# One sum of squares in the first mixer's opening, and three reordered mixers, in a six-stage block on one core

## The chip, the cores and the metric

The kernel runs on one core of one Trainium2 chip. The metric is the device time of one execution in microseconds (us). A core has five engines with a queue of instructions each: TensorE (PE: matmuls, PEld: the weight loads that go with them), VectorE (DVE), ScalarE (ACT), GpSimd (POOL) and SyncE (SP), which starts the DMAs here. Each engine runs its own queue strictly in order and waits on semaphores for the others.

## The reference, cut to what matters

The input x is 512 tokens by 1024 channels in float32. It goes through six stages, each of the form x = x + rmsnorm(stage(rmsnorm(x))):

```
even : retention (4 heads) and stick-breaking attention (8 heads), gated, projected back
odd  : hgrn2 (4 heads, chunked decays) and a convolution + RG-LRU recurrence, gated, projected
diff : differential attention (8 score units per pair of heads), a 31-tap depthwise conv + layernorm
ffn0 : gated feed-forward, 1024 -> 2816 -> 1024
ssm  : a diagonal complex state-space scan and latent attention (6 heads)
ffn1 : as ffn0
rms_norm(x) = x * rsqrt(mean(x*x over channels) + 1e-6) * w
```

The four stages that are not feed-forward are the mixers.

## The kernel before, in words

x lies channel-major: eight blocks (k = 0 to 7) of 128 channels by 512 tokens. Every projection is a product of a 128 by 128 weight tile with such a block, made at nearly full precision from three fp32r matmuls: high by high, high by low and low by high (L889 to L891; in the openings L906, L910, L917). High parts are rounded by ACT (`hh` from x, L1059; `wh` from the raw weights, L1034), low parts are the differences, made by DVE (`hl`, L1125) and POOL (`wl`, L3165, four instructions for a slot). Weights come as a stream of slots of eight tiles (512 KB). Slot n is loaded by SP, rounded by ACT, split by POOL; rings of three slots hold `raw`, `wh` and `wl`, so a step that starts a slot (`STARTS`) also makes ACT round, and POOL split, the slot two places on.

A stage's opening takes the blocks of x as they come. For block k, ACT makes `hh` and the square of x (L1064), DVE makes `hl`, PE does the stage's first three or four products with this block. The norm's factor is applied later, when results leave PSUM, so the products need not wait for it. For the factor, the squares must be summed over all channels: PE multiplies by a 128 by 128 matrix of ones (plain float32) into bank 7, and ACT then takes Ln and Exp (`rs`, L1067, L1069); the evictions `e` by DVE wait for that. There are two forms of this sum:

- the stages named in `ADDING` (odd, ffn0, ssm, ffn1): the squares go to `y` in the arena, DVE adds them up there (steps `sa` 1 to 7, L1132), and PE multiplies the one total (L978);
- the other stages (even, diff): PE multiplies each square by itself, eight matmuls that add up in bank 7 (L988). In even they stand in groups of four, three and one, behind the products of blocks 3, 6 and 7 (`SQUARES`), and the squares lie in four buffers of `nrm`.

The order of all this is written out by hand: `steps_even()` and its fellows list the steps of a stage, every engine walks the same list and emits its own part of each step. On top of that a table, `AHEAD`, moves single steps ahead of others: an entry `(step, of)` takes `step` out and puts it directly before `of`. It had 79 entries for even, 158 for odd, 214 for diff and 146 for ssm. A move changes the place of the step in every queue at once, and with it the order in which that engine reaches its waits.

Steps that come up below. In odd: `hf`/`hq` are projections; `fa`, `fb`, `fc` turn hf into log decays (ACT L1943 to L1947 and L1954 to L1959, DVE L1799 to L1803); `bd 3` loads ACT's sigmoid table (L1894) and sets a mask on DVE (L1716, L1718); `lf` is DVE L1783; `t` are the 8 by-token products of the values (L960 to L962), the first of which needs PSUM banks 0 to 3, thus the evictions of hq by DVE (L1691); `h0` and `hl` are the score products by head and level (L1636), which need DVE (L1809, L1833, L1815) and POOL (L2037). In diff: `ra` and `rb` rotate q and k (PE L2116, DVE L2208 and L2214, POOL L2408), `r1` are scores (L2131) that need the rotated k, `fn` is the conv branch's norm and gate (DVE L2278, L2280, L2283). In ssm: `an` is a block of six POOL instructions on angles (L3115 to L3125).

Of the kernel before, what the change touches and what calls it, by code (L numbers as in the profile page):

```python
# [18 lines left out]
KT = D // 128  # L19
# [114 lines left out]
SQUARES = {3: (0, 1, 2, 3), 6: (4, 5, 6), 7: (7,)}  # L134
# [6 lines left out]
def opening(gs):  # L141

    even = gs == OPENS["even"]

    def at(kind, k):
        return [(kind, k) if even or k >= NB else (kind, k, 1)] if k < KT else []

    out = at("nx", 0) + at("hi", 0) + at("nx", 1)
    for k in range(KT):
        out += at("lo", k) + at("hi", k + 1) + at("nx", k + 2)  # L150
        out += [("w", g, k) for g in gs]
        if gs in LATER:
            out += ADDED.get(k, [])
        else:
            out += [("sq", n) for n in (SQUARES.get(k, ()) if even else (k,))]
    return out + [("rs",)] * (gs not in LATER)
# [6 lines left out]
ADDING = ("odd", "ffn0", "ssm", "ffn1")  # L163
# [54 lines left out]
def steps_even():  # L218
    sq, sk = ([(g, j) for j in range(4)] for g in ("sq", "sk"))
    out = opening(OPENS["even"]) + merge(group(sq[3], 8), [("e", g) for g in sq[:3]]) + [("e", sq[3]), ("rt",)] + groups(sk, 8, "e")  # L220
# [168 lines left out]
def steps_ssm():  # L389
# [29 lines left out]
    for n in range(0, 24, 2):  # L419
# [78 lines left out]
    "diff": [  # L498
# [292 lines left out]
def program(nc, io):  # L791
    with ExitStack() as ctx:
# [61 lines left out]
        def square_at(stage):  # L854
            return [y[:, k, :] for k in range(KT)] if stage in ADDING else sqr + [nrm[:, 4, :], nrm[:, 5, :]] if stage == "even" else sqr
# [109 lines left out]
        def pe_norms(e, stage, step):  # L965
# [7 lines left out]
            elif kind == "sq":  # L973
# [7 lines left out]
                if k == 0:  # L981
                    claim(e, 7)
                    if stage == "even":
                        e.wait_ge(s_mats, 16)
# [2366 lines left out]
```

## Time and profile before

| | us |
|---|---|
| median of 3 runs (1749.95 to 1752.95) | 1750.78 |
| the profiled execution | 1755.67 |
| its span, first to last instruction | 1753.9 |
| PE busy in it | 1699.9 |
| DVE / ACT / POOL busy | 961.7 / 769.7 / 949.0 |

Read from it first who is busy (PE, by far), then whose waits cost: only time in which PE idles, or runs at the lower granted clock, can be won without taking work off PE. Stages follow each other: odd runs from about 304 to 546 us, diff from 546 to 791, ssm from 1148 to 1372.

### The profile page before, as it was taken

The page shows a single profiled execution, that of the slowest core. Times are in us where ns is not written, and L with a number is a line of the kernel's source. Part 1 is how long each engine was busy: PE and PEld are TensorE (multiplying, and loading weights), DVE is VectorE, ACT ScalarE, POOL GpSimd, SP SyncE. Part 2 cuts the span into 40 slices and gives each one's busy share as a digit, 9 for nine tenths or more (in the row PEclk, how much of TensorE's full clock was granted, in tenths as well). Part 3 has the DMA queues.
Part 4 walks back from the last instruction along what each step waited for, and adds up shares of the span by engine and source line. Part 5 has one row for each costly group of instructions (what it writes and reads, how often), then busy time and mean ns, then how long its engine had stood idle before and what let it go on. Part 6 is the DMA issues. An engine that isn't in the chain of part 4 may idle for free.

```text
span 1753.9 us, 21148 instructions
## 1 busy us (share of the span) xinstructions
PE 1699.9 (97%) x7871; PEld 1324.0 (75%) x7871; DVE 961.7 (55%) x1504; ACT 769.7 (44%) x1314; POOL 949.0 (54%) x1108
## 2 busy tenths in 40 slices
PE   9999999998999999899999999999999999999997
PEld 6767668776878776687888888875457888888886
DVE  2033555779966898747614313369786752132344
ACT  4254675477475334754322222354335533222232
POOL 4433224678964463235656656569354565565662
PEclk9999999999999999899999999999999999999998
DMA  5221112222112221022322222221001222222221
GB/s 210 83 84 61 36 49 96 95 73 84 49 37 86 83 85 49 26 83 97 108 97 96 96 96 97 96 72 48 13 24 49 85 96 101 92 97 100 96 96 69
DMA packets 39702, 139.96 MB, mean 80 GB/s; under 512 B 4528, under 2 KB 4656, under 8 KB 39472
## 3 DMA queue, kind: packets, MB, share of 16 engines
q1 hardware_dynamic: 39600, 138.61, 23.4%
q8 instruction: 63, 1.03, 0.2%
q14 instruction: 39, 0.32, 0.1%
HBM read 136.50 MB, written 2.10 MB: 79 GB/s over the span
## 4 chain that ended last, share of the span: by engine, by line
PE 81%; DVE 11%; ACT 4%; issue 2%; POOL 1%; DMA 0%; SPq 0%; DVEq 0%; ACTq 0%
PE ps L889 19%; PE ps L891 18%; PE ps L890 18%; PE ps L910 1%; PE ps L960 1%; PE ps L917 1%; PE ps L962 1%; PE ps L961 1%; DVE ps L1101 1%; PE ps L1178 1%; PE ps L1176 1%; PE ps L1177 1%; PE ps L906 1%; PE ps L1312 1%; PE ps L1636 1%
## 5 line engine op out<-in xcount | busy, mean ns | idle before, releaser
L3165 POOL TENSOR_TENSOR wl<-raw,wh 128x256 fp32r<-128x256 f32 x988 | 801.3, 842 | 710.0 <-ACT wh L1034 704.0
L1034 ACT ACTIVATE wh<-raw 128x1024 fp32r<-128x1024 f32 x246 | 259.4, 1056 | 479.9 <-PE ps L891 441.0
L889 PE MATMUL ps<-hh,wh 128*128 128x512 f32 x1028 | 414.6, 403 | 2.4 <-ACT arena L1472 0.8
L891 PE MATMUL ps<-hh,wl 128*128 128x512 f32 x1028 | 401.3, 390 | 0.0
L890 PE MATMUL ps<-hl,wh 128*128 128x512 f32 x1028 | 401.0, 390 | 0.0
L889 PEld LDWEIGHTS ps<-hh,wh 128*128 128x128 f32 x1028 | 193.5, 188 | 56.2 <-issue 12.0
L890 PEld LDWEIGHTS ps<-hl,wh 128*128 128x128 f32 x1028 | 193.5, 188 | 42.8 <-issue 4.5
L891 PEld LDWEIGHTS ps<-hh,wl 128*128 128x128 f32 x1028 | 193.4, 188 | 41.0
L889 PE MATMUL ps<-mh,wh 128*128 128x512 f32 x540 | 220.0, 407 | 3.4 <-DVE ml L2955 1.4
L891 PE MATMUL ps<-mh,wl 128*128 128x512 f32 x540 | 211.2, 391 | 0.0
L890 PE MATMUL ps<-ml,wh 128*128 128x512 f32 x540 | 210.9, 391 | 0.0
L889 PEld LDWEIGHTS ps<-mh,wh 128*128 128x128 f32 x540 | 102.0, 189 | 32.9 <-issue 3.3
L891 PEld LDWEIGHTS ps<-mh,wl 128*128 128x128 f32 x540 | 101.6, 188 | 21.7
L890 PEld LDWEIGHTS ps<-ml,wh 128*128 128x128 f32 x540 | 101.9, 189 | 21.1 <-issue 2.2
L2469 DVE TENSOR_TENSOR ml<-arena,mh 128x512 fp32r<-128x512 f32 x44 | 36.3, 825 | 101.2 <-ACT mh L2500 101.2
L2458 DVE TENSOR_TENSOR arena<-ps,nrm 128x512 f32<-128x512 f32 x44 | 30.3, 688 | 107.0 <-PE ps L891 107.0
L2456 DVE TENSOR_TENSOR arena<-ps,nrm 128x512 f32<-128x512 f32 x44 | 29.9, 680 | 107.1 <-PE ps L891 94.3
L2238 DVE SCALAR_TENSOR_TENSOR ps<-arena,vec,ps 128x512 f32<-128x512 f32 x116 | 79.9, 748 | 0.2
L1125 DVE SCALAR_TENSOR_TENSOR hl<-x,vec,hh 128x512 fp32r<-128x512 f32 (+1 forms) x63 | 45.1, 720 | 28.2 <-ACT hh L1059 28.2
L1076 ACT ACTIVATE nrm<-arena 128x256 f32<-128x256 f32 (+1 forms) x68 | 34.1, 501 | 56.2 <-DVE arena L1142 56.0
L960 PE MATMUL ps<-wh,hh 128*128 128x512 f32 x128 | 52.2, 408 | 2.8 <-DVE arena L1691 1.9
L1176 PE MATMUL ps<-mh,wh 128*128 128x256 f32 x184 | 53.1, 289 | 0.0
(497 smaller groups left out, 2746.7 us busy)
## 6 DMA issues: line engine op xcount, KB each, us to landing
raw<-in_w SPq DMA_DIRECT2D x246, 512.0 KB, 3.3
x<-in_x SPq DMA_DIRECT2D x8, 256.0 KB, 8.3
out<-x SPq DMA_DIRECT2D x8, 256.0 KB, 2.0
arena<-in_rope SPq DMA_DIRECT2D x3, 512.0 KB, 4.7
arena<-in_dec SPq DMA_DIRECT2D x1, 1024.0 KB, 6.3
mats<-in_mats SPq DMA_DIRECT2D x1, 576.0 KB, 9.4
raw<-in_w SPq DMA_DIRECT2D x2, 256.0 KB, 3.7
arena<-in_lw SPq DMA_DIRECT2D x1, 512.0 KB, 4.1
```

Source lines behind the costliest of these rows:

```text
L889: e.matmul(ps[b][:], a, xh, start=first, stop=False)
L890: e.matmul(ps[b][:], a, xl, start=False, stop=False)
L891: e.matmul(ps[b][:], l, xh, start=False, stop=final).then_inc(pe.sem, pe.up(*step))
L960: e.matmul(ps[i][:], hh[:, k, cut(i)], a, start=(k == 0), stop=False)
L1034: e.activation(wh[:, n % NHL, :], raw[:, n % NRAW, :], ACT.Copy).then_inc(rounded.sem, rounded.up(n))
L1076: e.activation(sqr[d % 2][:, c], y[:, d, c], ACT.Square).then_inc(act.sem, act.up("oe", d, *half))
L1125: e.scalar_tensor_tensor(out=hl[:, k, c], in0=x[:, k, c], scalar=V(PRE[stage], k), in1=hh[:, k, c].bitcast(F32), op0=MUL, op1=SUB).then_in ...
L1176: e.matmul(ps[b][:, cols(h)], a, mh[:, r, cols(h)], start=(k == 0), stop=False)
L2238: e.scalar_tensor_tensor(out=yb[:, j, :] if q == 30 else conv_in[j], in0=du[:, j, q:q + T], scalar=V("dww", 4 * q + j), in1=conv_in[j], op ...
L2458: e.tensor_tensor(f_up[f % 2], ps[bank(stage, ("fu", f))][:], rb_pre, MUL).then_inc(dve.sem, dve.up("e", ("fu", f)))
L2469: e.tensor_tensor(ml[:, i, :], f_up[f % 2], mh[:, i, :].bitcast(F32), SUB).then_inc(dve.sem, dve.up("mixed", f))
L3165: e.tensor_tensor(wl[:, n % NHL, cut(i, 2)], raw[:, n % NRAW, cut(i, 2)], wh[:, n % NHL, cut(i, 2)].bitcast(F32), SUB).then_inc(split.sem, ...
```

## The change

First, even joins the stages in `ADDING`. Its squares go to the arena, DVE adds them up, and PE multiplies once by ones. The steps `sa` stand as in the other stages: `sa 1` behind block 3, `sa 2` behind block 5, `sa 3` to `sa 7` behind block 7. `sq 7` and `rs` follow directly on the opening. In odd, ffn0, ssm and ffn1 a group of eight products stands between the last `sa` and `sq 7`; in even none does. Second, the tables of moves of odd, diff and ssm are other ones (184, 243 and 164 entries); that of even stays. The stream of weights and every operation of the three mixers stay the same, only their order in the queues differs (and with it where ACT's tables are loaded).

```diff
-SQUARES = {3: (0, 1, 2, 3), 6: (4, 5, 6), 7: (7,)}
 ADDED = {3: [("sa", 1)], 5: [("sa", 2)], 7: [("sa", k) for k in range(3, KT)]}
...
         if gs in LATER:
             out += ADDED.get(k, [])
         else:
-            out += [("sq", n) for n in (SQUARES.get(k, ()) if even else (k,))]
+            out += [("sq", k)]
...
-ADDING = ("odd", "ffn0", "ssm", "ffn1")
+ADDING = ("even", "odd", "ffn0", "ssm", "ffn1")
...
-    out = opening(OPENS["even"]) + merge(group(sq[3], 8), [("e", g) for g in sq[:3]]) + ...
+    out = opening(OPENS["even"]) + [("sq", KT - 1), ("rs",)] + merge(group(sq[3], 8), [("e", g) for g in sq[:3]]) + ...
...
     "odd": [
-        (('w', ('p', 6), 3), ('hn3', 2)), (('hn4', 1), ('w', ('p', 6), 2)), (('hn4', 0), ('hn4', 1)), (('hn3', 1), ('w', ('p', 6),
...
-            return [y[:, k, :] for k in range(KT)] if stage in ADDING else sqr + [nrm[:, 4, :], nrm[:, 5, :]] if stage == "even" else sqr
+            return [y[:, k, :] for k in range(KT)] if stage in ADDING else sqr
...
                 if stage in ADDING:
                     claim(e, 7)
+                    if stage == "even":
+                        e.wait_ge(s_mats, 16)
+                        e.wait_ge(consts.sem, consts[EXACT[-1]])
                     e.wait_ge(dve.sem, dve["sa", k])
                     e.matmul(ps[7][:], M("ones"), y[:, 0, :], start=True, stop=True).then_inc(pe.sem, pe.up("sq", k))
```

**Place one, the opening of even.** PE before, behind the products of block 5: the products of block 6, three sums, the products of block 7, the last sum, and then group sq 3 (L889 on).

```order
L906 MATMUL ps<-hh,wh 128x512 x3
L910 MATMUL ps<-hl,wh 128x512 x3
L917 MATMUL ps<-hh,wl 128x512 x3
L988 MATMUL ps<-nrm,mats 128x512 x3
L906 MATMUL ps<-hh,wh 128x512 x3
L910 MATMUL ps<-hl,wh 128x512 x3
L917 MATMUL ps<-hh,wl 128x512 x3
L988 MATMUL ps<-nrm,mats 128x512
L889 MATMUL ps<-hh,wh 128x512
```

PE now at the same place (line numbers have moved by about 20):

```order
L926 MATMUL ps<-hh,wh 128x512 x3
L930 MATMUL ps<-hl,wh 128x512 x3
L937 MATMUL ps<-hh,wl 128x512 x3
L926 MATMUL ps<-hh,wh 128x512 x3
L930 MATMUL ps<-hl,wh 128x512 x3
L937 MATMUL ps<-hh,wl 128x512 x3
L1001 MATMUL ps<-arena,mats 128x512
L909 MATMUL ps<-hh,wh 128x512
```

Seven of the eight sums are gone, and the one that is left reads the arena. DVE before, from its first instruction on, and then now:

```order
L3141 MEMSET small 128x1 x3
L1337 MEMSET nrm 128x256
L1125 SCALAR_TENSOR_TENSOR hl<-x,vec,hh 128x512 x8
L1350 SCALAR_TENSOR_TENSOR mh_scratch<-ps,nrm 128x512 x4
L1137 COPY small<-ps 128x4
```

```order
L3160 MEMSET small 128x1 x3
L1356 MEMSET nrm 128x256
L1144 SCALAR_TENSOR_TENSOR hl<-x,vec,hh 128x512 x4
L1151 TENSOR_TENSOR arena<-arena 128x512
L1144 SCALAR_TENSOR_TENSOR hl<-x,vec,hh 128x512 x2
L1151 TENSOR_TENSOR arena<-arena 128x512
L1144 SCALAR_TENSOR_TENSOR hl<-x,vec,hh 128x512 x2
L1151 TENSOR_TENSOR arena<-arena 128x512 x5
L1369 SCALAR_TENSOR_TENSOR mh_scratch<-ps,nrm 128x512 x4
```

Seven adds have come in, five of them in a row behind the last `hl`.

**Place two, ACT in odd, where the log decays are made.** Before, from the table load of `bd 3` on:

```order
L1894 ACT_TABLE_LOAD
L1943 ACTIVATE nrm<-arena 128x512
L1945 ACT_TABLE_LOAD
L1945 ACTIVATE nrm<-nrm 128x512
L1947 ACT_TABLE_LOAD
L1947 ACTIVATE nrm<-nrm,small 128x512
L1936 ACTIVATE mh<-mh_scratch 128x512
L1034 ACTIVATE wh<-raw 128x1024 x2
L1954 ACT_TABLE_LOAD
L1954 ACTIVATE arena<-arena,small 128x512
L1955 ACTIVATE nrm<-nrm,small 128x512
L1957 ACTIVATE nrm<-nrm 128x512
```

Now, from the last `fa` on (L1962 to L1966 are the former L1943 to L1947, L1973 to L1978 the former L1954 to L1959):

```order
L1962 ACTIVATE nrm<-arena 128x512
L1964 ACTIVATE nrm<-nrm 128x512
L1966 ACTIVATE nrm<-nrm,small 128x512
L1053 ACTIVATE wh<-raw 128x1024
L1973 ACTIVATE arena<-arena,small 128x512
L1974 ACTIVATE nrm<-nrm,small 128x512
L1976 ACTIVATE nrm<-nrm 128x512
L1978 ACTIVATE nrm<-nrm,small 128x512
L1955 ACTIVATE mh<-mh_scratch 128x512
L1053 ACTIVATE wh<-raw 128x1024 x2
L1973 ACTIVATE arena<-arena,small 128x512
```

`bd 3` now stands among the tanh steps `lt`, ahead of `la`, and with it the eight loads between here and the first `hd` are gone.

**Place three, DVE in diff, where the last q and k are rotated.** Before (L2208 and L2214 are `ra` and `rb`, the first of each q, the second k; L2246 belongs to the softmax rows):

```order
L2208 TENSOR_TENSOR arena<-arena 128x512
L2278 TENSOR_TENSOR arena<-arena,nrm 128x512
L2280 TENSOR_SCALAR arena<-arena,vec 128x512
L2283 SCALAR_TENSOR_TENSOR arena<-arena 128x512
L2214 TENSOR_TENSOR arena<-ps,arena 128x512
L2278 TENSOR_TENSOR arena<-arena,nrm 128x512
L2280 TENSOR_SCALAR arena<-arena,vec 128x512
L2278 TENSOR_TENSOR arena<-arena,nrm 128x512
L2280 TENSOR_SCALAR arena<-arena,vec 128x512
L2208 TENSOR_TENSOR arena<-arena 128x512
L2214 TENSOR_TENSOR arena<-ps,arena 128x512
```

Now (19 is to be added to the line numbers):

```order
L2227 TENSOR_TENSOR arena<-arena 128x512
L2265 TENSOR_REDUCE small<-ps 128x1 x2
L2227 TENSOR_TENSOR arena<-arena 128x512
L2297 TENSOR_TENSOR arena<-arena,nrm 128x512
L2299 TENSOR_SCALAR arena<-arena,vec 128x512
L2233 TENSOR_TENSOR arena<-ps,arena 128x512
L2297 TENSOR_TENSOR arena<-arena,nrm 128x512
L2299 TENSOR_SCALAR arena<-arena,vec 128x512
L2302 SCALAR_TENSOR_TENSOR arena<-arena 128x512 x2
L2233 TENSOR_TENSOR arena<-ps,arena 128x512
```

Between the two `rb` stood two rounds of `fn` 0 and one `ra`; now one round of `fn` 0 and two `fn` 2 stand there. On PE the product `ra` of k followed directly on that of q; now a score unit and the first values (`r1 11`, `v1 0`) stand between them. In ssm, POOL's last five blocks `an` 3 to 7 now follow each other without a weight split in between, and the split of the slot that begins with tile (p 2, 2) comes behind `an 7`; before it came ahead of `an 6`.

## Rows read from the trace of the kernel before

**Rows 1.** The page: busy time and share by engine; the chain's shares.

```profile
PE 1699.9 (97%) x7871; PEld 1324.0 (75%) x7871; DVE 961.7 (55%) x1504; ACT 769.7 (44%) x1314; POOL 949.0 (54%) x1108
PE 81%; DVE 11%; ACT 4%; issue 2%; POOL 1%; DMA 0%; SPq 0%; DVEq 0%; ACTq 0%
```

**Rows 2.** Windows of odd, diff, ssm: length, busy by engine, granted clock, DMA.

```profile
304.00:546.00 242.00, 232.94 (x1183) 191.53 (x1183) 192.84 (x274) 150.60 (x262) 175.15 (x183) 0.99 0.20 68
546.00:791.00 245.00, 233.54 (x1082) 174.45 (x1081) 191.15 (x338) 123.37 (x245) 100.66 (x127) 0.98 0.21 69
1148.00:1372.00 224.00, 210.59 (x982) 140.25 (x983) 171.91 (x249) 103.03 (x211) 128.34 (x118) 0.98 0.13 43
```

**Rows 3.** The chain of waits in even's opening: start us, length us, what.

```profile
17.78 3.43 PE ps L988 x8
21.21 0.69 PE ps L906 x3
...
27.36 2.58 PE ps L988 x6
...
32.00 0.86 PE ps L988 x2
```

**Rows 4.** Timeline of the opening: start, length, engine, line, what, idle before.

```profile
12.72 3.76 POOL L3165 TENSOR_TENSOR wl<-raw,wh 128x256 fp32r<-128x256 f32 x4 [3.64 <-ACT wh L1034]
...
18.67 0.63 ACT L1064 ACTIVATE nrm<-x 128x512 f32<-128x512 f32 x1 [1.35 <-PE ps L988]
...
22.22 0.75 DVE L1125 SCALAR_TENSOR_TENSOR hl<-x,vec,hh 128x512 fp32r<-128x512 f32 x1 [0.38 <-ACT hh L1059]
...
23.61 1.04 ACT L1034 ACTIVATE wh<-raw 128x1024 fp32r<-128x1024 f32 x1
...
24.73 5.57 POOL L3165 TENSOR_TENSOR wl<-raw,wh 128x256 fp32r<-128x256 f32 x8 [4.67 <-ACT wh L1034]
```

**Rows 5.** The adds of squares: all 28 (ns min/median/max), then from the timeline.

```profile
L1132 DVE TENSOR_TENSOR arena<-arena x28: 682/1038/1240, 307.7 to 1399.5; 128x512 f32<-128x512 f32 x28
1395.10 5.49 DVE L1132 TENSOR_TENSOR arena<-arena 128x512 f32<-128x512 f32 x5
```

**Rows 6.** PE's waits in odd, 304 to 546 us: total, times, longest.

```profile
PE ps L1636 <- POOL mh_scratch L2037: 1.9, 1, 1.9
PE ps L960 <- DVE arena L1691: 1.9, 1, 1.9
...
PE ps L1636 <- DVE arena L1833: 1.0, 2, 0.8
PE ps L1636 <- DVE arena L1809: 0.8, 1, 0.8
```

**Rows 7.** Timeline of DVE and ACT in odd.

```profile
390.96 0.68 DVE L1783 TENSOR_TENSOR ml<-mh_scratch,mh 128x512 fp32r<-128x512 f32 x1
391.69 0.48 DVE L1716 MEMSET arena<- 128x512 f32 x1
...
397.42 1.28 ACT L1894 ACT_TABLE_LOAD   x1
398.71 0.63 ACT L1943 ACTIVATE nrm<-arena 128x512 f32<-128x512 f32 x1
...
418.74 1.28 ACT L1974 ACT_TABLE_LOAD   x1
```

**Rows 8.** Windows at the lower clock in odd: columns as in rows 2.

```profile
399.20:402.60 3.40, 3.40 (x9) 2.66 (x10) 3.25 (x4) 3.34 (x5) 3.40 (x4) 0.51 0.04 11
436.80:440.20 3.40, 3.40 (x9) 2.65 (x8) 3.24 (x6) 1.74 (x3) 3.40 (x4) 0.50 0.19 77
```

**Rows 9.** Timeline of PE and DVE in diff.

```profile
708.69 1.12 PE L2116 MATMUL ps<-arena,mats 128*128 128x512 f32 x2 [0.78 <-ACT arena L2390]
...
715.00 1.13 PE L2131 MATMUL ps<-arena 64*128 64x512 f32 x4 [2.24 <-POOL arena L2408]
709.27 1.37 DVE L2280 TENSOR_SCALAR arena<-arena,vec 128x512 f32<-128x512 f32 x1
```

**Rows 10.** Timeline of POOL and PE in ssm.

```profile
1296.50 1.43 POOL L3115 TENSOR_TENSOR hh_scratch<-arena 128x512 f32<-128x512 f32 x1 [12.94 <-DVE hh_scratch L2921]
...
1303.59 1.28 POOL L3125 TENSOR_TENSOR hl_scratch<-hl_scratch,nrm 128x512 f32<-128x512 f32 x1
1315.88 0.48 PE L889 MATMUL ps<-mh,wh 128*128 128x512 f32 x1
```

More of the change, by code:

```diff
@@ L219, in steps_even @@
     sq, sk = ([(g, j) for j in range(4)] for g in ("sq", "sk"))
-    out = opening(OPENS["even"]) + merge(group(sq[3], 8), [("e", g) for g in sq[:3]]) + [("e", sq[3]), ("rt",)] + groups(sk, 8, "e")
+    out = opening(OPENS["even"]) + [("sq", KT - 1), ("rs",)] + merge(group(sq[3], 8), [("e", g) for g in sq[:3]]) + [("e", sq[3]), ("rt",)] + groups(sk, 8, "e")
     out += [("t", "sv", k) for k in range(8)] + [("te", "sv", i) for i in range(4)]
@@ L982, in pe_norms @@
                     claim(e, 7)
-                    if stage == "even":
-                        e.wait_ge(s_mats, 16)
-                if stage == "even" and k == KT - 1:
-                    e.wait_ge(consts.sem, consts[EXACT[-1]])
                 e.wait_ge(act.sem, act["square", k])
```

290 rows, old and new, of the table AHEAD are left out of this document.

## The prediction

> **What bounds the kernel now.** I read the page first. PE is busy for 1699.9 of 1753.9 us, no other engine for more than 55%, and 81% of the chain that ended last is PE [rows 1]. So time is won in three ways only: PE work taken away, PE idle time closed, or PE time at the lower granted clock avoided. Next I cut the trace into windows by stage. PE idles 242.00 - 232.94 = 9.1 us in odd, 11.5 in diff and 13.4 in ssm [rows 2], in sum 34.0. That is all that the new tables can close, beside the clock. Then I read the chain through even's opening: it lies on PE from block 3 on, and the eight sums stand in it with 3.43, 2.58 and 0.86 us [rows 3]. Last came PE's waits in the three mixers, each followed back to its releaser in the timeline.
>
> **The opening of even.** Removed: seven of eight sums. All eight cost 3.43 + 2.58 + 0.86 = 6.87 us, 0.86 each, so 6.0 us of PE work go. All of it was on the chain.
>
> Added: seven adds on DVE and a wait of PE's one sum for the last of them. Behind that waiting sum on PE stands the group sq 3, and behind that the whole kernel, so each us of this wait counts in full. When does each side come?
> - PE: blocks 4 to 7 can start at 17.78, where the first sums stood. The matmuls of a block take three rows of 0.69 (one is shown [rows 3]), 2.06 us, so PE stands at the sum at 17.78 + 4 x 2.06 = 26.0.
> - ACT: its square of block 4 waited 1.35 us for a sum to free the buffer [rows 4]. Each square has its own place now, so that wait goes and ACT is 1.35 earlier from there on. The rounding of slot 3 comes at 22.3 in place of 23.61, and POOL's split of that slot starts at 23.4.
> - DVE: the last `hl` ended at 22.97 [rows 4]. It could be 1.35 earlier (21.6), but `sa 2` now stands in between; I put its end at 21.9. Five adds in a chain follow. An add takes 0.68 us at best and 1.04 in the median, and a row of five took 5.49 us, 1.1 each [rows 5].
>
> The fast adds of this trace lie where POOL does nothing and the slow ones beside POOL's splits. With two adds ahead of POOL's start at 23.4 (0.79 each from start to start) and three beside it (1.14 each), the last ends at 21.9 + 1.6 + 3.4 = 26.9. The sum then runs from 27.0 to 27.9; before, the last sum ended at 32.00 + 0.86 = 32.86. Gain: **5.0 us**, that is 6.0 less a new wait of 1.0.
>
> The next product needs slot 3 split in full: 23.4 + 2.8 (half of the 5.57 for two slots) = 26.2, or 27.2 at the slower rate of 3.76 [rows 4]. Both are ahead of 27.9. Bounds: if no add meets POOL, PE does not wait, and the gain is 6.0. If all five take 5.49 in sum and the split starts as late as before (24.73) and at 3.76, it ends at 28.5, and the gain is 32.86 - 28.5 = 4.4. Evictions, Ln and Exp move ahead with the sum, and what follows in even keeps its order, so nothing there gives the 5.0 back.
>
> The Trainium skill (SBUF — State Buffer, Who interferes with whom) says that a DVE instruction with two SBUF inputs contends with a GpSimd instruction that reads SBUF, as an exclusive lock where the loser blocks fully. The trace agrees as to who meets whom (682 against 1038 and 1240 ns [rows 5]), but an add that waited out a whole split instruction of 0.7 us would take 1.4 us. By that, three such adds would end about 0.9 us later and the gain would be 4.1; I keep the measured rate.
>
> **Odd, the new table.**
> - The first by-token product waited 1.9 us for the eviction of hq 2 [rows 6]. On DVE `lf 0` (0.68) and `bd 3` (0.48 and a little) stood ahead of that eviction [rows 7]; both now stand elsewhere, while the rest of the work ahead of it is the same. Gain 1.2.
> - Eight table loads, the first at 397.42 and the last at 418.74, 1.28 us each [rows 7], take 10.3 us of ACT just where the decays are made on which the first `hl` products wait. Those wait 1.9 + 1.0 + 0.8 = 3.7 us [rows 6]. Seven loads are gone and that of `bd 3` is elsewhere, and eight products now stand ahead of the first `hl`. Gain 3.7, if nothing else is late; bounds 0 and 3.7.
> - Two stretches of 3.4 us run at 1.2 GHz instead of 2.4, after PE waits just ahead of them [rows 8]. Each costs 1.7. I count the second as gone (1.7), the first as still there, since 0.7 of its wait stays.
> - Against it: `rt` stands one product (0.68) earlier and waits that much longer for Exp, +0.7. And a new order has new waits of its own: I take +1.4, between 0 and the 9.1 that the stage now has, near the longest single one.
>
> Sum for odd: -1.2 - 3.7 - 1.7 + 0.7 + 1.4 = **-4.5**.
>
> The Trainium skill (ScalarE: Activation LUTs, What ACT_TABLE_LOAD costs) gives 1283 ns for a load and 1380 ns of drain besides. The trace has the load, but the next activation starts at 398.71, 0.01 us behind it [rows 7]. By the rule, ACT would win 21.3 us here; PE's gain would still be the 3.7, since these waits are all there is.
>
> **Diff.** PE waited 0.78 us with `ra` of k and 2.24 us with `r1 12` [rows 9]. The row of the first names ACT L2390, which had nothing to do with it: `ra` of k claims the bank that `rb` of q frees on DVE. A score unit and a value product now lie in between, and this wait goes. The second was for POOL's rotation of k, behind two rounds of `fn` 0 on DVE, of which one took 0.68 + 1.37 [rows 9]. One such round is replaced by two `fn` 2 of 0.7 each, so DVE is freed by only about 0.7 us, and I count 1.0. New waits: +0.8. Sum **-1.0**, bounds -11.5 and +5.
>
> **Ssm.** I find nothing here that clearly goes. DVE puts the softmax rows ahead of part of the scan and other parts of the scan ahead of them. **0**, bounds -6 (about half of the 13.4 idle) and +6.
>
> **Sum.** -5.0 - 4.5 - 1.0 + 0 = -10.5. The profiled execution took 1755.67 us (span 1753.9 and 1.8 around it), which would become 1745.2. It lies 4.9 above the median of the runs, 1750.78, so for the runs I forecast 1750.8 - 10.5 = **1740.3**.
>
> **The rivals.**
> - The tables give nothing in sum: what closes in odd opens elsewhere. For it: odd, diff and ssm keep the same work and the same dependences, and in ssm I find no gain. Against: ACT's 10.3 us of loads do go. Time 1750.8 - 5.0 = 1745.8.
> - The tables give far more: in each of the three mixers half the idle time closes (17.0) and half of the lower clock with it (three stretches, 5.1), less the 3 to 6 that is in doubt. For it: the waits are many and short, which is what an order can cure. Against: most of them sit between steps that depend directly on each other. Time about 1750.8 - 5.0 - 15 = 1730.8; a half-way case gives 1735.
> - The tables take back what the opening gives: two or three new waits of the size of the longest now, 2.2, each with a stretch at the lower clock (1.7), make 3 x 3.9 = 11.7 against 5.5 gained. Time about 1750.8 - 10.5 + 11 = 1751.3, no change.
> - Slower: in ssm POOL's `an 7` waits for DVE's scan (12.94 us before [rows 10]), and the split of the slot that begins with tile (p 2, 2) now stands behind it. Before, `an 7` ended at 1304.9 and PE reached that tile at 1315.88 [rows 10]. With 2.8 for the split, PE does not wait unless `an 7` comes more than 8.2 us later relative to PE. For slower than now by 4 us the stall must be 14.5, so `an 7` 22.7 us late, two of its blocks and more. For it: the five blocks stand in a row. Against: two of them used to wait for DVE anyway. Time 1755 or more.
>
> **How the numbers follow.** This kernel's measurement can tell 0.2% (3.5 us) from no change. Chances: the forecast 0.50; nothing from the tables 0.22; far more 0.11; taken back 0.12; slower 0.05. Faster by over 0.2%: all of the first and the third, 0.20 of the second's 0.22 (at 1745.8 it is 5 us off) and a little of the fourth, 0.82. Within 0.2%: the rest of the second and most of the fourth, 0.12. Slower: 0.06. The range takes the forecast with 1.0 on either side for the opening and 6 for the tables: 1740.3 less 7 is 1733, and on the other side it takes in the second rival and stops at 1749.
>
> **What would show it.** In the new profile: even's one sum starts at 27 us or so, with about 1 us of idle PE ahead of it put down to DVE's adds, and sq 3 starts at 28; at 26 with no wait, the adds met no POOL work. ACT shows no table load between the last `fa` and the first `hd` of odd. The waits of L1636's successor (L1655) on POOL and DVE are below 2 us in sum, and PE idles under 6 us in odd. In diff, the wait of the scores on POOL's rotation is 1.2 or less. In ssm idle PE stays at 13 us within 3. The prediction is wrong if idle PE in the three mixers is not some 4 to 6 us below 34.0, or if the tile (p 2, 2) shows a wait for POOL's split.

## The result, and the profile after

The changed kernel takes 1731.19 us, the median of 4 runs (1729.30 to 1732.52), against 1751.61 us (4 runs, 1749.95 to 1752.95): ratio 0.9883, 95% interval 0.9866 to 0.9900. That is 20.4 us faster, where 10.5 were forecast, and 1.8 us below the forecast range. A second set of runs gave 1731.58 us and 0.9878 (0.9864 to 0.9891). The profiled execution took 1732.52 us.

From the page of the changed kernel, busy time and the chain's shares (as [rows 1]):

```profile
PE 1684.2 (97%) x7857; PEld 1317.2 (76%) x7857; DVE 949.8 (55%) x1511; ACT 764.1 (44%) x1309; POOL 951.2 (55%) x1108
PE 85%; DVE 9%; ACT 3%; issue 2%; DMA 1%; SPq 0%; POOL 0%; DVEq 0%; ACTq 0%
```

PE is busy 15.7 us less, of which the seven sums are 6.0. DVE got seven adds more and is still busy 11.9 us less. Odd, diff and ssm, cut at the places that answer to [rows 2], same columns (length, PE, PEld, DVE, ACT, POOL, granted clock, DMA share, GB/s):

```profile
298.90:535.10 236.20, 229.28 (x1182) 189.69 (x1183) 183.97 (x274) 144.48 (x257) 179.00 (x182) 1.00 0.21 70
535.10:776.30 241.20, 232.18 (x1082) 173.20 (x1081) 190.20 (x338) 123.74 (x245) 99.53 (x127) 0.99 0.21 70
1133.40:1348.30 214.90, 205.59 (x982) 138.79 (x982) 163.13 (x249) 103.19 (x210) 123.61 (x118) 0.99 0.13 45
```

The three stages are 5.8, 3.8 and 9.1 us shorter. PE idles 6.9, 9.0 and 9.3 us in them, in sum 25.3 against 34.0. So 8.7 of the 18.7 us are idle time. In the other 10.0 PE is busy less with the same matmuls, and most of that is the clock: three stretches of 3.4 us at 1.2 GHz stand in these stages where eight stood, and five times 1.7 us are 8.5. The rows show five of the eight; two more are in [rows 8], and one follows directly on the stretch at 716.70. A second profiled execution of the changed kernel has only one such stretch, so their number is not fixed by the order alone. Before, then now:

```profile
703.00:706.40 3.40, 3.40 (x5) 1.71 (x6) 2.19 (x4) 3.27 (x6) 0.00 (x0) 0.50 0.00 0
716.70:720.10 3.40, 3.11 (x9) 1.55 (x9) 3.40 (x6) 3.20 (x8) 0.00 (x0) 0.50 0.00 0
1232.10:1235.50 3.40, 2.83 (x8) 0.85 (x10) 2.85 (x8) 2.53 (x7) 0.65 (x1) 0.50 0.01 2
1252.60:1256.00 3.40, 3.40 (x9) 1.27 (x8) 2.56 (x5) 0.00 (x0) 0.00 (x0) 0.50 0.00 0
1283.30:1286.70 3.40, 3.40 (x6) 1.27 (x5) 2.70 (x5) 1.19 (x3) 0.26 (x1) 0.50 0.00 0
```

```profile
689.90:693.30 3.40, 3.40 (x11) 1.67 (x10) 1.06 (x3) 1.78 (x4) 0.00 (x0) 0.50 0.00 0
703.50:706.90 3.40, 3.40 (x9) 1.71 (x9) 2.71 (x6) 3.40 (x8) 0.00 (x0) 0.50 0.01 2
1191.60:1195.00 3.40, 3.40 (x4) 0.93 (x4) 2.90 (x5) 0.00 (x0) 1.75 (x3) 0.50 0.21 55
```

The opening, from the chain of waits of the changed kernel (start, length, what; answers to [rows 3]):

```profile
20.90 0.74 DVE hl L1144
21.64 0.61 DVE arena L1151
22.34 0.70 DVE arena L1151
23.14 1.05 DVE arena L1151
24.29 1.05 DVE arena L1151
25.43 1.04 DVE arena L1151
26.60 1.10 PE ps L1001 x2
```

The chain has left PE there and runs over the last `hl` and five adds: two of 0.7 us, both begun before POOL starts a split at 22.62, and three of 1.05 beside it. The sum starts at 26.60 after a wait of 1.25 us.

### The profile page after: what moved, and what is told of

Same layout as the page of the kernel before. It is cut to its first block, busy times and chain, and to the rows that moved or that the text cites. A ratio compares the mean times of both kernels' runs of the same rounds, so it can differ in the third digit from the quotient of the medians.

```text
span 1730.3 us, 21127 instructions
## 1 busy us (share of the span) xinstructions
PE 1684.2 (97%) x7857; PEld 1317.2 (76%) x7857; DVE 949.8 (55%) x1511; ACT 764.1 (44%) x1309; POOL 951.2 (55%) x1108
## 4 chain that ended last, share of the span: by engine, by line
PE 85%; DVE 9%; ACT 3%; issue 2%; DMA 1%; SPq 0%; POOL 0%; DVEq 0%; ACTq 0%
PE ps L909 20%; PE ps L911 19%; PE ps L910 19%; PE ps L980 2%; PE ps L982 2%; PE ps L981 2%; PE ps L1655 1%; DVE ps L1120 1%; PE ps L1197 1%; PE ps L1195 1%; PE ps L1196 1%; PE ps L930 1%; DVE ps L2257 1%; PE ps L937 1%; PE ps L1331 1%
## 5 line engine op out<-in xcount | busy, mean ns | idle before, releaser
L1197 PE MATMUL ps<-mh,wl 128*128 128x256 f32 x184 | 52.0, 283 | 0.0
```

What stands on the lines that cost most here:

```text
L1197: e.matmul(ps[b][:, cols(h)], l, mh[:, r, cols(h)], start=False, stop=(k == len(OUT_ROWS[stage]) - 1)).then_inc(pe.sem, pe.up(*(of if h el ...
```

## The experiments

All ratios are to the kernel before, on the same chip. Differences in us are of medians unless called means, those to the changed kernel to its second set of runs (1731.58). The runs of some experiments come from another chip than that set; the medians of the kernel before lie between 1751.76 and 1752.82 on the four chips. "Stage time" is from a stage's first to its last matmul that signals, in the profiled execution. A theory or rival with a letter is one of those named in the expectation just above it.

### The parts alone, and the tables together

Four kernels carry one part each, a fifth the three tables with the old opening. For the odd table, for instance:

```diff
     "odd": [
-        (('w', ('p', 6), 3), ('hn3', 2)), (('hn4', 1), ('w', ('p', 6), 2)), ...
+        (('hn4', 2), ('w', ('p', 7), 2)), (('w', ('p', 6), 3), ('hn4', 2)), ...
```

**Opening only.** 

> Only the opening of even is changed; the tables of odd, diff and ssm are those of the kernel before. Account from the two traces (theory A): the kernel's own PE work falls by 6.0 us, one new wait of 1.25 us comes in, and small gaps go, so -5.4 us, a time near 1746. Rival B (the opening sets free more than its own stage): -9 or more, because later waits and low-clock stretches move too. Rival C (the added adds cost more elsewhere): -3 or less. The three mixers should show the same waits as before, so idle PE in them stays at 32.7 us within 0.5; whether the low-clock stretches (8 of 3.4 us in the profiled execution before) stay 8 shows whether they hang on the waits alone or also on when a wait comes.

**Odd only.** 

> Only odd's table of moves is the new one. Theory A (each table's gain is its own closed idle time, 9.06 to 6.96 us, plus 1.7 us for each low-clock stretch that goes, two there): -2.1 from waits and 0 to -3.4 from the clock, so -2 to -5.5. The prediction's account: -4.5 with idle time below 6 us. Rival B (the tables only pay off together): 0 within 1.

**Diff only.** 

> Only diff's table is the new one. Theory A: idle PE in diff falls from 10.05 to 7.6 us and three low-clock stretches become two, so -2.5 to -4. The prediction's account: -1.0. Rival B (only together): 0 within 1, or slower.

**Ssm only.** 

> Only ssm's table is the new one. Theory A: idle PE in ssm falls from 13.6 to 9.5 us, 1.4 us of PE time beside it goes, and up to two low-clock stretches (1.7 each) go, so -5.5 to -9. The prediction's account: 0 within 6. Rival B (only together, or an artefact of when the stage starts): 0 within 1. If A holds for all four, their sum is -18 to -24 and meets the -20.4 us of the whole change.

**Tables only.** 

> The three new tables with the old opening of even. Alone, odd's, diff's and ssm's gave -5.9, -4.5 and -9.9 us (medians), in sum -20.3; the whole change gives -20.4 to -20.9, of which the opening alone gives -5.2. Theory A (the opening adds fully, the tables overlap by some 4 us among themselves, as low-clock stretches can go only once): -15.5 to -17. Rival B (the tables add fully, and the opening's gain is what is lost with them): -19 to -21.

**The changed kernel again.** 

> The changed kernel itself, once more, beside the others of this call. The four parts alone gave -5.0, -5.8, -4.7 and -9.4 us as means against the kernel before, in sum -24.9, where the whole gave -20.4. Theory A (the parts add up and the difference is spread of the runs): -21 to -25 here. Rival B (the gains overlap, because low-clock stretches can go only once): -20.5 again, within 1.

| | median | ratio | 95% | mean against 62 executions of before |
|---|---|---|---|---|
| opening only | 1747.62 | 0.9971 | 0.9960 to 0.9983 | -4.6 |
| odd only | 1746.90 | 0.9968 | 0.9955 to 0.9980 | -5.3 |
| diff only | 1748.35 | 0.9974 | 0.9963 to 0.9985 | -4.2 |
| ssm only | 1742.89 | 0.9944 | 0.9931 to 0.9958 | -9.0 |
| tables only | 1734.03 | 0.9902 | 0.9889 to 0.9915 | -18.2 |
| changed, again | 1731.58 | 0.9878 | 0.9864 to 0.9891 | -20.7 |

By means, each known to some 0.7, the tables alone sum to -18.5 and together give -18.2. If each mean is taken against the kernel before on the same chip only, it is -19.9 against -18.0, the sum known to about 1.4. So the tables add up within the noise; an overlap of some 4 us is not there, one of 1 or 2 us can't be told. The opening gives 4.6 alone and 2.5 on top of the tables; that difference is at the edge of what the runs tell. Ssm's table, on which I had put 0, is the largest part.

The opening-only kernel shows something about the clock. The first by-token product of odd waits as long in it as before ([rows 6]), yet the clock stays at 2.4 GHz behind it. Its wait in PE's timeline, and the window behind it (granted clock 1.00, against 0.51 in [rows 8]):

```profile
394.57 0.50 PE L959 MATMUL ps<-wh,hh 128*128 128x512 f32 x1 [1.86 <-DVE arena L1689]
```

```profile
394.60:398.00 3.40, 3.40 (x15) 2.84 (x16) 3.25 (x4) 3.35 (x4) 3.40 (x4) 1.00 0.05 8
```

So the same wait has a low-clock stretch behind it in one execution and none in another. And odd, without its two stretches, took 243.62 us of stage time in place of 244.64, not 3.4 less: PE idled 10.7 us where it had idled 9.1.

### Ssm: which part of its table

```diff
# POOL's blocks moved; in the kernel before
+ (('an', 3), ('qa', 1)), (('an', 4), ('r4', 5)), (('an', 5), ('vw', 2)),
+ (('an', 6), ('vw', 2)), (('an', 7), ('s3b', 3))
# put back; in the changed kernel
+ (('an', 3), ('e', ('un', 1))), (('an', 4), ('r2', 5)), (('an', 5), ('r2', 13)),
+ (('an', 6), ('r1', 14)), (('an', 7), ('r2', 16))
```

**Blocks moved.** 

> The kernel before; in ssm only POOL's five angle blocks (an 3 to an 7) are moved to where the new table has them, about. Measured so far: the new ssm table alone gives -9.4 us; DVE's 245 instructions of the stage take 9 us less in it, since the scans and products of DVE (2.06 to 2.23 us beside a block an, 1.20 alone) meet POOL less often. Theory A (POOL's blocks beside DVE's scan cost the time): the moved blocks alone give -3 to -9 us and DVE's busy time in ssm falls by 5 or more. Rival B (the gain is the softmax rows' new order, the contention is a bystander): 0 within 1.5, or slower.

Measured 1745.59 us, ratio 0.9965 (0.9952 to 0.9979), so -6.4 us; ssm's stage time is 216.1 against 220.0 to 221.6 in the four unmodified profiles. The ssm window, same columns:

```profile
1143.50:1363.00 219.50, 209.67 (x982) 140.93 (x981) 166.60 (x250) 102.33 (x209) 125.57 (x119) 0.98 0.13 44
```

DVE is busy 166.60 us, 5.3 less than in [rows 2]. Five POOL blocks in other places are worth two thirds of the table. PE's waits for DVE there (0.9 for L2861, 0.9 for L2921) are gone. The run can't tell by itself whether the blocks' time beside DVE or their order against the waits on them gives the gain.

**Blocks put back.** 

> The changed kernel with the same five blocks put back to where they stood before, beside the same neighbours. Theory A: DVE's busy time in ssm rises by 5 or more, and the time by +3 to +9 us against the changed kernel. Rival B: +1.5 or less.

Measured 1741.08 us, 0.9940 (0.9928 to 0.9952), so 9.5 us slower than the changed kernel. The size is the upper end of theory A's, the cause is not: DVE's busy time in the stage is within 1.3 us of the changed kernel's, where 5 or more had been expected. PE idles 15.8 us of the stage time in place of 9.5. DVE and then PE wait for a block that now stands late:

```profile
1265.06 0.69 DVE L2899 TENSOR_TENSOR hh_scratch<-ps,mh_scratch 128x512 f32<-128x512 f32 x1 [5.68 <-POOL ml_scratch L3144]
...
1267.28 1.01 PE L2683 MATMUL ps<-nrm,arena 128*128 128x128 f32 x3 [5.20 <-ACT arena L3064]
```

So the place of a block counts in two ways: who waits for it, and what it slows while it runs. The next two runs take the second by itself.

```diff
# in the kernel before, behind the last instruction of an 5 (its semaphores are left out here)
+ for m in range(6):
+     e.tensor_tensor(beside, c_, s_, ADD)
...
# the second kernel: ahead of them
+ e.wait_ge(dve.sem, dve["s_h", 3])
```

**Extra POOL work beside a full DVE.** 

> The kernel before, with six more adds on POOL (512 columns, two inputs in SBUF, the result is never read) directly behind block an 5 of ssm, in a stretch where POOL idles (1246 to 1254 us, 0.05 us busy) and DVE is busy for 8.00 of 8.00 us. No queue of weights or angles is held up: POOL's next work is the split at 1271. Theory A (POOL's work beside DVE's slows DVE, and DVE sets the pace there): DVE's busy time in ssm rises by 3 to 5 us and the time by +2 to +5 us. Rival B (what counts is only where blocks stand in POOL's queue): 0 within 1.

**The same work later.** 

> The same six adds, held back until DVE has finished s3b 3 (about 1262 us), so that they run from 1262 to 1270, where DVE is busy for 3.43 of 8.00 us and PE for all of them. Theory A: DVE's busy time rises by 1.5 or less and the time by +1 or less. If both this and the run beside DVE's full stretch cost the same, it is not DVE's pace that counts. Rival B: 0 within 1 in both.

Beside: 1755.62 us, 1.0019 (1.0009 to 1.0029), DVE's busy time in the stage 4.7 above the mean of the four unmodified profiles. Later: 1754.02 us, 1.0014 (1.0004 to 1.0024), DVE +2.6, more than expected; but the four unmodified profiles differ by 3.3 us among themselves. The times alone don't part the two. The traces show what happened at the place. Timeline with the work beside (DVE, the six POOL adds, PE):

```profile
1242.58 1.75 DVE L2914 TENSOR_TENSOR hl_scratch<-hl_scratch,mh_scratch 128x512 f32<-128x512 f32 x1
1244.25 0.68 DVE L2861 TENSOR_REDUCE small<-ps 128x1 f32<-128x512 f32 x1
...
1246.64 0.71 DVE L2920 SCALAR_TENSOR_TENSOR hl_scratch<-hl_scratch,ml_scratch 128x512 f32<-128x512 f32 x1
1247.27 1.75 DVE L2921 TENSOR_TENSOR hh_scratch<-hh_scratch,ml_scratch 128x512 f32<-128x512 f32 x1
...
1242.19 9.33 POOL L3129 TENSOR_TENSOR nrm<-mh_scratch,ml_scratch 128x512 f32<-128x512 f32 x6
...
1247.69 1.62 PE L2650 MATMUL ps<-arena 128*128 128x384 f32 x2 [4.25 <-ACT nrm L3033]
```

and with it later:

```profile
1261.24 8.42 POOL L3130 TENSOR_TENSOR nrm<-mh_scratch,ml_scratch 128x512 f32<-128x512 f32 x6 [16.28 <-DVE hh_scratch L2921]
...
1250.59 2.23 PE L2650 MATMUL ps<-arena 128*128 128x384 f32 x4 [2.19 <-ACT nrm L3033]
```

Two instructions of DVE with two inputs in SBUF take 1.75 us in place of 0.68, one that reads PSUM keeps 0.68, and PE's longest wait there is 4.25 us in place of 2.19. Nothing was reordered and no queue held up. A third one with two SBUF inputs (L2920) took 0.71 with the adds going on, and the starts say why: POOL's adds ran from 1242.19 to 1243.78, from 1245.54 to 1246.81 and from 1246.88 to 1248.47, and the three of DVE ended 0.55, 0.54 and 0.55 us after these ends. Each waited out the POOL instruction that was running when it began.

So in this execution the slowed instructions reach PE as a wait. How much that costs at the end the times resolve badly: the place costs 1.6 us by medians, 1.3 by means with a standard error of 0.9. Why the later kernel cost 2 us at all is open: its profiled stage time is within 0.3 us of the kernel before.

**Half of the new order.** 

> The changed kernel; ssm follows the new order up to tile (un 4, 1) (about 95 us into the stage) and the old order from there. The changed kernel stands at 1731.5, and without ssm's new table it would stand near 1741. Reading idle PE and low-clock stretches of the two traces, of ssm's -9 us some 7 lie ahead of that tile (in the first run of softmax units, r1 4 to r1 10, with the 2.1 us wait) and 2 behind. Theory A: 1732 to 1735. Rival B (a half order gives nothing, as one move alone gave +5.5 where -2 to -3.8 was expected): 1739 or more.

Measured 1733.81 us, 0.9896 (0.9883 to 0.9909): 2.2 us above the changed kernel. As theory A had it, most of the gain needs only the new order in the first 95 us of the stage.

**One move only.**

```diff
+ (('r1', 10), ('v2', 0))
```

> The kernel before, with one move more in ssm: the score unit r1 10 three products later. It waited 2.10 us for ACT's exponentials, the longest wait of ssm, and a low-clock stretch followed at once. Theory A (wait and stretch both go): -2 to -3.8 us against the kernel before. Rival B (what follows then waits in its place, since ACT's rows of the softmax set the pace): 0 to -1. Rival C: the wait goes, the stretch stays or moves: -1 to -2.

Measured 1757.95 us, 1.0033 (1.0022 to 1.0045): 5.5 us slower, and no theory had that. The 2.10 us wait went, and PE waits at the product before and at the scores after in its place:

```profile
1249.17 4.63 PE L2673 MATMUL ps<-arena 128*128 128x512 f32 x8 [3.98 <-DVE ml L2870]
...
1262.10 2.04 PE L2650 MATMUL ps<-arena 128*128 128x256 f32 x4 [2.25 <-ACT arena L3033]
```

PE reached a product that needs DVE and waited 3.98 us there, where it had not waited in the kernel before. And the scores, made later, came late: DVE stood idle from 1250.3 to 1259.03 until they were there for its next reduction, where its longest such wait had been 0.9 us. So the 2.10 us could not be won by moving this one step; the engines that feed PE set the pace there.

### Odd: the table loads

```diff
# in the changed kernel's odd table
+ (('bd', 3), ('fc', ('hf', 0)))
```

> The changed kernel with one step of odd, bd 3, put back among the log decays; nine table loads (1.28 us each) return on ACT there. Theory A (the loads were what the first hl products waited for, as the prediction put it, 3.7 us): +1.5 to +4 us against the changed kernel, as waits of the hl products or of the first hq evictions. Rival B (ACT has room there, the waits had another cause): 0 within 0.7.

Measured 1734.11 us, 0.9892 (0.9879 to 0.9905), so +2.5 us; odd's stage time goes from 238.7 to 243.3, more than the medians differ, and one low-clock stretch is in it that the changed kernel does not have there. PE's waits in odd, total, times, longest: put back, then the changed kernel.

```profile
PE ps L1655 <- DVE arena L1828: 2.9, 1, 2.9
PE ps L980 <- POOL wl L3184: 1.3, 1, 1.3
PE ps L909 <- ACT arena L1901: 1.1, 1, 1.1
```

```profile
PE ps L1655 <- DVE arena L1828: 1.6, 1, 1.6
PE ps L909 <- DVE small L1729: 1.1, 1, 1.1
PE ps L909 <- ACT arena L1901: 0.8, 1, 0.8
PE ps L1017 <- ACT small L1903: 0.8, 1, 0.8
PE ps L1655 <- DVE ml_scratch L1834: 0.8, 1, 0.8
```

This is theory A: the loads cost the first `hl` products 1.3 us of waiting, and by way of late weight roundings a `t` product another 1.3. The put-back kernel is not odd as it was, though: its odd stage has 18 table loads, the kernel before had 14 and the changed kernel has 9.

### The openings: two tries at more

```diff
-    ... [("sq", KT - 1), ("rs",)] + merge(group(sq[3], 8), ...
+    ... group(sq[3], 8)[:2] + [("sq", KT - 1), ("rs",)] + merge(group(sq[3], 8)[2:], ...
```

> The changed kernel, with two products of group sq 3 ahead of even's one sum. The sum waited 1.25 us for the last add. Theory A (the wait is the price of the missing cover): it goes and gives 0.5 to 1.2 us back, so 0.3 to 1.2 us faster than the changed kernel; the next products need slot 3, whose split ended near 26.3, so a wait of up to 0.5 may stand in its place. Rival B: ACT now rounds slot 5 ahead of the small matrices that the sum needs, so the same 1.2 us of idle time returns as a wait for ACT: 0 within 0.5.

Measured 1737.86 us, 0.9918 (0.9905 to 0.9931): 6.3 us slower than the changed kernel, beyond both theories. The timeline of ACT, POOL, PE and DVE:

```profile
25.19 1.06 ACT L1053 ACTIVATE wh<-raw 128x1024 fp32r<-128x1024 f32 x1 [4.90 <-PE ps L937]
...
28.26 8.30 POOL L3184 TENSOR_TENSOR wl<-raw,wh 128x256 fp32r<-128x256 f32 x12 [8.12 <-ACT wh L1053]
...
31.09 0.79 PE L909 MATMUL ps<-hh,wh 128*128 128x512 f32 x1 [6.00 <-POOL wl L3184]
...
21.28 3.86 DVE L1151 TENSOR_TENSOR arena<-arena 128x512 f32<-128x512 f32 x5
```

One rounding of ACT, which waits for PE to leave the opening, now stands ahead of two that could go at once, so POOL splits 5.6 us later. B named the right instruction and missed what was behind it. The last row tells something besides: five adds with POOL idle take 3.86 us; in the changed kernel, where the split starts beside the second, they take 4.90.

```diff
-ADDING = ("even", "odd", "ffn0", "ssm", "ffn1")
+ADDING = ("even", "odd", "diff", "ffn0", "ssm", "ffn1")
```

> The changed kernel, with diff's opening treated as even's: the squares are added by DVE, and PE sums once. PE loses 6.0 us of work again. But DVE has the former stage's norm to apply in this opening (2.1 us a block with hl, where PE takes 2.1), so the seven adds of 0.7 to 1.2 us delay it. Theory A (PE's work is what counts): -4 to -5.5 against the changed kernel. Rival B (DVE becomes the bound: last hl near 555.2 on the changed kernel's clock, adds to 559.3, sum to 560.2, where it now ends at 560.6): 0 to -1.5, with a wait of 3 us or more ahead of the sum.

Measured 1734.04 us, 0.9896 (0.9883 to 0.9908): 2.5 us slower than the changed kernel. DVE is the bound, as B said; PE's waits ahead of the sum and of `rt`:

```profile
559.91 1.10 PE L1001 MATMUL ps<-arena,mats 128*128 128x512 f32 x2 [2.55 <-DVE arena L1151]
...
562.54 0.88 PE L1017 MATMUL ps<-mats,nrm 128*128 128x128 f32 x3 [1.53 <-ACT nrm L1088]
```

The 6 us of PE work less were lost to waits, and in the profiled execution to low-clock stretches as well (three in diff; of the eight other profiles with this table six have none there, one has one, the changed kernel's has two). No kernel tried is faster than the changed one.

## Why the prediction was wrong

**The direction and the opening were right.** Forecast -5.0; alone it measures -4.6 (mean), and the sum starts at 26.60 with 1.25 us of wait, where 27.0 and 1.0 were forecast. Two adds of 0.7 us and three of 1.05 beside POOL came as worked out (1.15 from start to start, where 1.14 was taken). On top of the tables the opening gave only 2.5, which may be noise.

**Odd, forecast -4.5, measured -5.3.** The wait for the eviction of hq 2 is gone whole. No table load stands between the last `fa` and the first `hd`, and the loads' share is 2.5 us, not 3.7: the `hl` waits fell to 1.6 + 0.8 = 2.4 us, not below 2 as I had put it. New waits are 1.1 (a product of hq) and 0.8 us (one of gg), where 1.4 was taken, and `rt` waits 0.8. PE idles 6.9 us, not under 6. I had counted seven loads as gone; odd has five less (9 in place of 14), as three came in at other places. The terms err both ways and nearly cancel, so the closeness is partly luck; DVE, not named, is busy 8.9 us less.

**Diff, forecast -1.0, measured -4.2.** The wait for POOL's rotation is 0.8, within the 1.2 named, and one of 0.7 for ACT follows:

```profile
701.36 0.92 PE L2150 MATMUL ps<-arena 64*128 64x384 f32 x4 [0.83 <-POOL arena L2427]
...
703.33 1.10 PE L2150 MATMUL ps<-arena 64*128 64x512 f32 x2 [0.69 <-ACT ml_scratch L2352]
```

Idle time fell by 2.4 us, where the terms allowed 1.0. For the rest there is the clock, on which I had counted nothing in diff: three stretches stood there before, two in the changed kernel's profile, none in that of the diff-only kernel. No run takes the two apart.

**Ssm, forecast 0, measured -9.0: this step failed.** I looked for PE waits that clearly go, found each short and bound to its neighbour, and put the term at 0. That left out what makes PE wait. In the middle of ssm DVE is nearly full, and for a part of it POOL's blocks run beside it: in the window 1212 to 1233 DVE is busy 20.22 of 21.00 us (the fourth figure) and POOL 19.13 (the sixth); in 1246 to 1254 it is DVE 8.00 of 8.00 and POOL 0.05. Before, these two windows and DVE's second scan of a block (busy us, mean ns of one), then the same scan now:

```profile
1212.00:1233.00 21.00, 17.23 (x85) 10.90 (x86) 20.22 (x24) 8.10 (x22) 19.13 (x13) 0.98 0.08 25
1246.00:1254.00 8.00, 5.90 (x26) 3.62 (x28) 8.00 (x13) 2.53 (x6) 0.05 (x1) 0.91 0.00 0
```

```profile
L2906 DVE TENSOR_TENSOR_SCAN hl_scratch<-small,hl_scratch 128x512 f32<-128x512 f32 x8 | 13.8, 1738 | 0.0
```

```profile
L2925 DVE TENSOR_TENSOR_SCAN hl_scratch<-small,hl_scratch 128x512 f32<-128x512 f32 x8 | 10.7, 1332 | 0.0
```

The same 249 instructions of DVE take 163.13 us in place of 171.91 [rows 2]. I had this contention in hand in the opening [rows 5] and did not carry it to ssm. What the runs show is that the place of POOL's five blocks counts: moved alone they give 6.4 us, put back in the new order they cost 9.5. How they act is shown in part only. The put-back kernel loses by waits for a late block, with DVE's busy time as before; the kernel with extra work shows slowed DVE instructions that PE then waits for; how the 9.0 us divide between the two is open. My check "idle PE in ssm 13 within 3" failed (9.3), and so did that on the three mixers, "some 4 to 6 us below 34.0": it is 8.7 below. The rival on the other side, `an 7` ahead of a split, was rightly small: `an 7` ended at 1283.6 and the split behind it at 1286.3, and PE came to the tile some 8 us later, with no wait for POOL.

**The clock, forecast -1.7, was mis-sized, in two ways.** In the two profiled executions that are compared, five stretches are gone, not one. But 1.7 us is PE's loss in a stretch, not the kernel's. Over 159 executions of the 16 kernels run here, 0.001 of mean granted clock goes with 0.92 us (standard error 0.08) among the executions of one kernel, and one stretch is 0.00097 of it. Mean clock rose from 0.9911 to 0.9949, some 3.9 stretches, so by this relation about 3.5 us of the 20.9 (mean of all eight executions). This is a correlation; no run switched a stretch on or off by itself. That the rest of a stretch comes back as longer waits elsewhere fits what the opening-only kernel showed in odd.

**The rivals.** "Tables nothing" (0.22) is refuted by the tables' 0.9902. "Far more" (0.11) had the time, 1730.8, but not the account: it wanted 17.0 us of idle time closed and three stretches gone, and 8.7 us and five came. Its sum was off as well: 17.0 + 5.1 less 3 to 6 is 16.1 to 19.1, not 15, which would be 1726.7 to 1729.7. So its hit is luck in part. I had argued that most waits sit between steps that depend directly on each other. They do, but how late the other engine is can change without any step of the pair being moved. That is what my sum could not see, and the range stopped at 1733 for the same reason.

## What to carry to other kernels

Cut the span into short windows and look for the engine that is busy all of one, even if its share of the whole is 55%: there its long instructions can be the cost, and PE's waits only show it. Compare the shortest and the mean duration of its instructions, and look at what POOL does beside the longest. Removing one wait where another engine sets the pace moves it, and can cost more than it held; before a step is moved, look at what each engine then queues ahead of what.

## What was not expected of the hardware

- DVE beside POOL: an instruction with two SBUF inputs takes up to 1.75 us in place of 0.68, a scan 1.5 to 2.2 in place of 1.2, and one that reads PSUM stays at 0.68. The time is not spread evenly: in the trace of the kernel before, of the 165 TENSOR_TENSOR of DVE with SBUF inputs alone that took 0.9 us or more, 142 ended 0.53 to 0.57 us after the POOL instruction that was running when they began. Most of the others work on 256 columns and ended 0.28 us after it. So what counts is how much of POOL's instruction is left. POOL pays too: six adds of 512 columns took 9.33 us beside a full DVE, 8.42 beside a half idle one.
- A wait of PE of 1.85 us had a stretch at 1.2 GHz behind it in one kernel, and the same wait of 1.86 us none in another. Two profiled executions of the changed kernel have three such stretches and one. Executions of one kernel differ as well: mean clocks from 0.989 to 0.994 in the kernel before.
- A stretch at the lower clock goes with about 0.9 us at the end, half of the 1.7 that it costs PE (a correlation over 159 executions).
